# Standing the filler matmuls of six RWKV steps in twos, in another set of places

## The reference, cut to what matters

```python
proj = h @ w_in[l]                       # r, k, v, the low-rank inputs and the gates are columns of this
def step(state, inp):                    # one token; 16 heads of 64 channels
    r_t, w_t, k_t, v_t, kk_t, a_t = inp
    sa = einsum('bhij,bhj->bhi', state, -kk_t)
    state = state * w_t + sa[..., None] * (kk_t * a_t) + v_t[..., None] * k_t
    return state, einsum('bhij,bhj->bhi', state, r_t)
```

## Time and profile before

| | us |
|---|---|
| median of 3 runs | 1886.01 (1885.96 to 1886.76) |
| profiled execution, whole | 1888.21 |
| profiled execution, span from first to last instruction | 1886.4 |
| mean granted TensorE clock | 0.984 |
| the six steps with three halves, together | 330.0 |

### The profile page before, as it was taken

How to read it: one execution, slowest core, us unless ns; L and a number is a source line. 1 busy time by engine, 2 the same in 40 slices (tenths; PEclk the granted TensorE clock), 3 DMA queues, 4 the chain that set the end, 5 groups by cost and what they waited for, 6 DMA issues and landing times.

```text
span 1886.4 us, 22629 instructions
## 1 busy us (share of the span) xinstructions
PE 1809.9 (96%) x9636; PEld 1482.6 (79%) x9636; DVE 829.4 (44%) x1206; ACT 768.5 (41%) x1126; POOL 514.0 (27%) x115
## 2 busy tenths in 40 slices
PE   6998998999999998998999999999999999999997
PEld 5896766888888787887888888787777788888886
DVE  2015526777877765434113344515864321113243
ACT  5235555556656643234223222434663342222222
POOL 2331200000000000342434444333334334444442
PEclk8999998999999999999999999999999999999999
DMA  4631222010001002432222222221213232222221
GB/s 159 217 116 46 79 87 64 26 48 26 26 28 44 23 34 80 155 134 101 89 99 103 89 98 103 90 99 68 71 64 112 78 112 90 97 104 90 98 103 67
DMA packets 54663, 161.19 MB, mean 85 GB/s; under 512 B 3327, under 2 KB 30335, under 8 KB 39844
## 3 DMA queue, kind: packets, MB, share of 16 engines
q1 hardware_dynamic: 42476, 135.40, 20.7%
q10 hardware_dynamic: 12088, 24.35, 3.8%
HBM read 153.16 MB, written 10.25 MB: 87 GB/s over the span
## 4 chain that ended last, share of the span: by engine, by line
PE 82%; DVE 8%; ACT 4%; issue 4%; DMA 1%; POOL 0%; ACTq 0%; DVEq 0%
PE ps L583 22%; PE ps L585 21%; PE ps L584 21%; PE ps L995 2%; PE ps L992 1%; DVE ht_lo L1888 1%; PE ps L1072 1%; PE ps L983 1%; PE ps L905 1%; PE ps L1036 1%; PE ps L910 1%; PE ps L703 1%; DVE x_res L1905 1%; ACT y_tok L1275 1%; PE ps L713 1%
## 5 line engine op out<-in xcount | busy, mean ns | idle before, releaser
L574 POOL TENSOR_TENSOR w_lo<-w_raw,w_hi 128x2048 fp32r<-128x2048 f32 x111 | 513.8, 4629 | 1341.9 <-ACT w_hi L1258 1341.9
L583 PE MATMUL ps<-ht_hi,w_hi 128*128 128x512 f32 (+1 forms) x1304 | 526.3, 404 | 21.8 <-DVE ht_lo L1888 10.9
L585 PE MATMUL ps<-ht_hi,w_lo 128*128 128x512 f32 (+1 forms) x1304 | 501.9, 385 | 0.0
L584 PE MATMUL ps<-ht_lo,w_hi 128*128 128x512 f32 (+1 forms) x1304 | 501.3, 384 | 0.0
L1258 ACT ACTIVATE w_hi<-w_raw 128x2048 fp32r<-128x2048 f32 x126 | 241.2, 1916 | 468.0 <-PE ps L585 414.3
L583 PEld LDWEIGHTS ps<-ht_hi,w_hi 128*128 128x128 f32 x1304 | 250.4, 192 | 82.0 <-issue 26.7
L585 PEld LDWEIGHTS ps<-ht_hi,w_lo 128*128 128x128 f32 x1304 | 250.0, 192 | 48.8
L584 PEld LDWEIGHTS ps<-ht_lo,w_hi 128*128 128x128 f32 x1304 | 250.8, 192 | 39.6 <-issue 1.7
L2342 DVE TENSOR_TENSOR hid_lo<-hidden,hid_hi 128x1024 fp32r<-128x1024 f32 x27 | 129.3, 4789 | 149.1 <-ACT hid_hi L1714 149.1
L583 PE MATMUL ps<-w_hi,hid_hi 128*128 128x512 f32 x432 | 168.2, 389 | 0.0
L585 PE MATMUL ps<-w_hi,hid_lo 128*128 128x512 f32 x432 | 168.1, 389 | 0.0
(11 more groups left out here) (308 smaller groups left out, 2569.6 us busy)
## 6 DMA issues: line engine op xcount, KB each, us to landing
w_raw<-in_wpack SPq DMA_DIRECT2D x114, 1024.0 KB, 4.8
w_raw<-in_wpack SPq DMA_DIRECT2D x24, 512.0 KB, 5.3
bias_skewed_dram<-bias_rows_dram ACTq DMA_DIRECT2D x1, 3840.0 KB, 23.0
toe<-bias_skewed_dram ACTq DMA_DIRECT2D x1, 3072.0 KB, 12.9
x_res<-in_x SPq DMA_DIRECT2D x4, 512.0 KB, 5.1
merged<-gate_dram ACTq DMA_DIRECT2D x2, 1024.0 KB, 9.1
gate<-gate_dram ACTq DMA_DIRECT2D x1, 2048.0 KB, 8.8
x_res<-in_x ACTq DMA_DIRECT2D x1, 2048.0 KB, 8.7
```

The lines of the kernel that those rows point to most:

```text
L574: nc.gpsimd.tensor_tensor(Wl[:, slot, :], raw[:, slot, :], f32(Wh[:, slot, :]), ALU.subtract).then_inc(lo_ready, 1)
L583: mm(dst, wh, ah, start=first, stop=False)
L584: mm(dst, wh, al, start=False, stop=False)
L585: return mm(dst, wl, ah, start=False, stop=last)
```

## The change

One tuple of numbers is replaced. It moves filler pieces among the places of the six steps that use it; their number (24) and everything else on every engine stays.

```diff
-SLOTS3 = (0, 2, 2, 1, 1, 1, 1, 0, 1, 1, 1, 1, 1, 2, 1, 1, 1, 2, 1, 1, 2)
+SLOTS3 = (0, 2, 2, 2, 0, 0, 2, 0, 0, 2, 0, 0, 2, 2, 2, 0, 2, 2, 0, 2, 2)
```

## The result

The changed kernel takes 1892.47 us (median of 18 runs, 1885.23 to 1895.03) against 1886.9 us of the kernel before (18 runs, 1885.84 to 1888.84): ratio 1.0029, 95% interval 1.0022 to 1.0035, so 5.5 us slower (4.2 to 6.6). The forecast was 4.5 us slower.

The account below looks back on a forecast made before the run. PE's own stream was taken to bound the kernel. Steps 0, 2, 4 at 0.8 us, 1 and 3 at 0.7, and 6 at 0.7 gave 4.5 us longer, 1890.5 us against the median; range 1884.0 to 1894.5.

Parts of the forecast that it names:

- The bound: Six changed steps: PE's own stream sets the time; in step 4 PE is busy 54.57 of 55.11 us.
- Chunk 2 to chunk 3: Slots 3 to 9: PE waits 0.8 to 0.9 us for chunk 2's state; `chunk_solve(3)` 0.38 late, 0.05 in steps 1, 3.
- The last output: Slots 10, 11 emptied: `to_tokens` waits 0.3 to 0.4 us for ACT's copy; at `variance` 0.3 late, 0.15 in step 3.
- The grams: Slot 15 emptied: `grams(1)` stays 2.2 us behind `grams(0)`, waiting for DVE's copies; +0.55 us per step, the largest term.
- Slots 17 to 20: Slot 18's piece goes to slot 19: 0 in five steps, +0.25 us in step 6.
- Starting a run: Seven filler runs joined in six steps: about 0.1 us saved each, 4.2 us, bounds 0 and 7.6.
- the rule on weight loads: Skill rule on PE: next weight load overlaps running matmuls, so joining saves nothing; forecast said its sum would be 4.2 higher.
- the joins pay: Rival, chance 0.12: no new waits in the six steps; 6.3 us saved, 4.2 of it by joining, giving 1879.7 us.
- The sum: Six steps: 0.8 us each in steps 0, 2, 4; 0.7 in 1, 3 and 6; 4.5 us longer.
- The rival of the clock: Rival, chance 0.08: new waits among small matmuls drop PE's clock; 1894 us if three steps fall, 1897.7 if all six.

Follow-up runs that it names:

- The joined kernel: Changed kernel with slot 16's pair ahead of `grams(1)`, slot 12's ahead of `to_tokens`, DVE's low part behind level 4's mask in steps 0, 2, 4: 1882.95 us, ratio 0.9981.
- after: The profile of the changed kernel, nothing else altered; that profiled execution took 1885.23 us, the least of its 18.
- the profiles of 1893.7 and 1888.21 us: The changed kernel measured once more, unaltered (1893.7 us, ratio 1.0038), and the profiled execution of the kernel before (1888.21 us).
- the kernel with the pair ahead: Changed kernel with slot 16's two pieces between `level_x(6)` and `grams(1)` instead of behind `grams(1)`: ratio 0.9998 to the kernel before.

## Why the prediction was right, and what was mis-sized

**The bound.** Right: PE's busy time in the five steps did not change, and the idle time that came in is the loss.

**Chunk 2 to chunk 3.** Right in kind and nearly in size. `chunk_solve(3)` lies 24.44 us behind the start of step 4, 24.12 before: 0.32 late, 0.38 forecast; 0.08 in step 3, 0.05 forecast. The wait is 0.74 us, 0.8 to 0.9 forecast. That the low part on DVE is the cause, which the forecast read from the chain without idle time in the earlier trace rows (the note that it speaks of stands in the second row there), is shown by moving it: the wait goes.

**The last output.** `to_tokens` waits for ACT's copy as forecast, 0.32 us by the starts, 0.3 to 0.4 forecast; moving the pieces of slot 12 ahead of it takes this wait out of the list. At `variance` step 4 is 0.41 late, 0.3 forecast; the squares' wait before it is gone. Alone, the part costs 0.31 us over five steps, where the forecast's terms come to -0.04 (0.3 - 0.38 in three steps, 0.15 - 0.05 in two): this is the term that it had too small.

**The grams.** Right, and the largest term: `grams(1)` stays 2.18 us behind `grams(0)`, 2.2 forecast, where it was 2.30. 0.46 us from `variance` to `norm_roots` against 0.55 forecast; alone, the part costs 0.54 to 0.60 per step, 3.4 us in all six with 0.60 in step 6.

**Slots 17 to 20.** Right: 0.00 in steps 0 to 4, and 0.28 in step 6 with slot 18's piece moved alone, 0.25 forecast.

**Starting a run, the term that was mis-sized.** The forecast took 0.1 us for each of 42 joins, 4.2 us, from the lone piece of slot 5 in the earlier trace rows against the long run in the earlier trace rows. The joined kernel shows about 0.03, and a loss in steps 1 and 3. What the lone piece costs more than 0.70 is then no price of filler: a change of stage is paid without filler as well. `level_x(2)` costs 0.50 behind `chunk_out` in after (576.17 to 576.67) and 0.40 behind a piece in the earlier trace rows (`level_x(3)`, 586.08 to 586.48). The bound of 0 that the forecast kept was the nearer one. The 4.2 us are no term of its sum: it lets the savings go where a wait follows. So its remark that by the rule on weight loads the sum would be 4.2 us higher does not follow from its own working. The rival "the joins pay" had no ground either: it counted 4.2 us for the joins of six steps, and with every wait covered they give about 0.5 over five.

**The sum.** The five steps lost 4.35 us and the forecast has 3.8 for them. Of the difference 0.35 is the output's term above and 0.23 the grams' (2.83 measured alone; the sum takes 0.5 in three steps, though its term says 0.55), and the levels are right (1.22, and 1.24 forecast). How much of it is the price of starting runs no run separates. That the total came near the steps' 5.2 is in part luck: between the profiles of 1893.7 and 1888.21 us, the steps differ by 5.2, step 6 up to its second `chunk_rhs` by 1.5, the stretch ahead of step 0 by -1.9 and what lies behind step 6 by 0.6.

**The rule on weight loads.** The Trainium skill (TensorE: Matmul & The Clock Gate, Part 2, step 1) has the next weight load run under the matmul before it, which would leave nothing to save by joining. About 0.03 us per run agrees with that better than the 0.1 that the forecast preferred to it.

**The rival of the clock.** It did not happen in steps 0 to 4: 1.00 in all profiles, with idle times of up to 0.66 us in the list. In step 6 it falls in the one profile of the kernel before and in one of the two of the changed kernel.

**What stays open.** The changed kernel's runs spread over 10 us and those of the kernel before over 3, and over 3.6 to 5.6 in the later rounds; and the kernel before with the low part moved gained 2.8 and 3.8 us where its steps show 1.3. A part of this is the clock in step 6: it did not fall there in any of the four profiles with the low part moved, in three profiles with the changed levels and the low part in its old place it cost 2.9 to 3.2 us (and nothing in the fourth, the first profile of the change), and in the kernel before, and in the three profiles with its levels in place, 1.6. With this 1.6 and the 1.3 of the steps the profiles account for 2.9 us, against 2.8 and 3.8 measured. It also means that the measured 5.5 us of the change need not be the steps' 5.2 alone: a deeper fall in step 6 may be in it, and the stretch ahead of step 0 differs from one execution to the next as well. Whether the order of work decides it or the moment at which step 6 begins was not tried.

## What to carry to other kernels

In a stream that is full, filler is worth only what it covers: put it in front of the instruction whose operand or PSUM bank another engine is still working on, not behind it, and count that chain (matmul's end, copies, restart) before moving it. Joining filler into longer runs saved next to nothing here; a place without filler pays the change between stages itself. Where a wait appears, look at the releaser's own queue first: moving one long instruction there, whose result is not needed yet, was worth more (1.3 us in the steps) than joining the filler with every wait covered (0.5).

## What the runs showed of the hardware

A list of idle times understates a wait on PE. The idle time ahead of L1072 is 0.66 us in the list. By the starts, `level_x(6)` to `grams(1)` takes 1.32 us, and the same run of `level_x(6)` behind `grams(0)` is followed after 0.50 where nothing waits (601.25 to 601.75 in the kernel with the pair ahead): 0.82. The difference of 0.16 is the end of the run: it is printed 0.66 long in both kernels, while the next start comes after 0.50. Against the kernel before it seems to be 0.84, but there the run stands behind filler and is printed 0.56. And a step of 55 us at full clock repeats within 0.05 us between executions, while whole executions of one kernel differ by 3 to 10: parts as small as 0.1 us per step could be told apart in single profiles where the medians of eleven runs could not.
